# Diagonal products of a state-space scan at full width: scaled x padded with zeros, two heads adding to one place

## What is computed

```python
xdt = xf * dtc[..., None]
decay = segsum_decay(a_cum)
cb = jnp.einsum('bclgn,bcsgn->bcgls', cc, bc)
y_diag = jnp.einsum('bcgls,bcgrls,bcsgrp->bclgrp', cb, decay, xdt)
...
y_off = jnp.einsum('bclgn,bcgrpn,bcgrl->bclgrp', cc, prev, jnp.exp(a_cum))
return (y_diag + y_off).reshape(b, l, h, p)
```

## Time and profile before

| | us |
|---|---|
| median of three runs | 1126.25 (1126.03 to 1126.39) |
| the profiled execution | 1126.33 |
| its span, first to last instruction | 1124.6 |
| TensorE busy | 1114.9 (99%) |
| VectorE busy | 859.2 (76%) |
| ScalarE busy | 565.1 (50%) |
| GpSimd busy | 38.4 (3%) |

### The profile page before, as it was taken

One profiled execution on the slowest core, in us unless ns is written; L12 is line 12 of the kernel. 1 busy time (PEld: TensorE's weight loads), 2 busy tenths in 40 slices (PEclk: granted clock), 3 DMA queues, 4 the chain that ended last, 5 costly groups with the idle time before them and its releaser, 6 DMA issues.

```text
span 1124.6 us, 15412 instructions
## 1 busy us (share of the span) xinstructions
PE 1114.9 (99%) x6378; PEld 968.7 (86%) x6378; DVE 859.2 (76%) x1011; ACT 565.1 (50%) x650; POOL 38.4 (3%) x93
## 2 busy tenths in 40 slices
PE   8999999999999999999999999999999999999997
PEld 7888888888888998899899888899899899888886
DVE  6778889999854798999998524598999999983325
ACT  5666676767533654454444322474545444442323
POOL 7000000000100000000000000000000000000000
PEclk9999999999999999999999999999999999999999
DMA  8244343443232332323323344212223323333221
GB/s 277 76 133 133 129 132 131 131 132 131 76 112 77 111 112 77 112 75 119 107 75 122 109 158 147 82 38 76 94 75 113 112 76 113 112 103 120 78 75 75
DMA packets 85414, 122.07 MB, mean 109 GB/s; under 512 B 4216, under 2 KB 71392, under 8 KB 85345
## 3 DMA queue, kind: packets, MB, share of 16 engines
q1 hardware_dynamic: 85162, 121.02, 32.8%
q10 hardware_dynamic: 182, 0.07, 0.0%
HBM read 118.92 MB, written 2.16 MB: 108 GB/s over the span
## 4 chain that ended last, share of the span: by engine, by line
PE 99%; DVE 0%; issue 0%; POOL 0%; ACT 0%; DVEq 0%; POOLq 0%
PE bank L1077 29%; PE bank L344 18%; PE bank L346 18%; PE bank L345 18%; PE bank L552 6%; PE bank L838 1%; PE bank L829 1%; PE bank L790 1%; PE bank L468 1%; PE bank L780 1%; PE bank L1460 1%; PE bank L1475 0%; PE bank L492 0%; PE bank L1477 0%; PE bank L1476 0%; PE bank L758 0%
## 5 line engine op out<-in xcount | busy, mean ns | idle before, releaser
L344 PE MATMUL bank<-h_hi,w_hi 128*128 128x512 f32 (+1 forms) x856 | 313.7, 366 | 0.0
L346 PE MATMUL bank<-h_hi,w_lo 128*128 128x512 f32 (+1 forms) x856 | 310.6, 363 | 0.0
L345 PE MATMUL bank<-h_lo,w_hi 128*128 128x512 f32 (+1 forms) x856 | 310.5, 363 | 0.0
L314 DVE TENSOR_TENSOR w_lo<-raw,w_hi 128x2048 fp32r<-128x2048 f32 x90 | 206.1, 2290 | 17.2 <-ACT w_hi L309 16.0
L309 ACT ACTIVATE w_hi<-raw 128x2048 fp32r<-128x2048 f32 x90 | 172.0, 1911 | 66.8 <-PE bank L346 65.9
L346 PEld LDWEIGHTS bank<-h_hi,w_lo 128*128 128x128 f32 x856 | 161.5, 189 | 25.9
L344 PEld LDWEIGHTS bank<-h_hi,w_hi 128*128 128x128 f32 x856 | 161.7, 189 | 25.0 <-issue 0.8
L345 PEld LDWEIGHTS bank<-h_lo,w_hi 128*128 128x128 f32 x856 | 161.8, 189 | 24.4
L571 DVE SCALAR_TENSOR_TENSOR tmp<-bank,par,tmp 128x511 f32<-128x511 f32 (+1 forms) x176 | 129.4, 747 | 17.3 <-ACT tmp L562 13.6
L1077 PE MATMUL bank<-w_hi,dn_hi 128*128 128x512 f32 x348 | 107.6, 390 | 0.0
L1440 DVE TENSOR_TENSOR dn_lo<-gated,dn_hi 128x1024 fp32r<-128x1024 f32 x22 | 26.9, 1224 | 105.4 <-ACT dn_hi L1436 105.4
(11 more groups left out here) (230 smaller groups left out, 1610.5 us busy)
## 6 DMA issues: line engine op xcount, KB each, us to landing
raw<-in_ffn_w_up SPq DMA_DIRECT2D x44, 1024.0 KB, 5.1
raw<-in_ffn_w_down SPq DMA_DIRECT2D x22, 1024.0 KB, 5.1
raw<-in_ssd_w_in SPq DMA_DIRECT2D x19, 1024.0 KB, 5.4
decay<-ac_dram SPq DMA_DIRECT2D x16, 512.0 KB, 5.2
raw<-in_ssd_w_out SPq DMA_DIRECT2D x8, 1024.0 KB, 5.0
from_start<-ac_dram SPq DMA_DIRECT2D x32, 128.0 KB, 4.5
xres<-in_x SPq DMA_DIRECT2D x4, 512.0 KB, 5.8
result<-xres SPq DMA_DIRECT2D x3, 512.0 KB, 2.6
```

The lines of the kernel that those rows point to most:

```text
L314: dve.tensor_tensor(lo[:], raw[n % 2][:], hi[:].bitcast(F32), ALU.subtract).then_inc(lo_ready, 1)
L344: pe.matmul(dst, wh, xh, start=first, stop=False, **kw)
L345: pe.matmul(dst, wh, xl, start=False, stop=False, **kw)
L346: return pe.matmul(dst, wl, xh, start=False, stop=last, **kw)
```

## The change

The tile `xdt` gets twice the columns: per chunk 256 in place of 128. Of these, columns 0 to 63 are head 0's scaled x, 64 to 191 stay zero, 192 to 255 are head 1's. A stationary operand is now 128 columns wide: head 0's x beside 64 zeros, or 64 zeros beside head 1's x. Each product writes all 128 partitions, and the second head's is added to the first's. GpSimd clears the middle columns once, behind its constants; VectorE waits for that before it writes pair 0. `heads_in` moves to another place in the memory, under `group_scale`.

```diff
-            xdt = sb("xdt", [P, T], scope=scope)
+            xdt = sb("xdt", [P, NCH, 2 * P], scope=scope)
...
+            with ExitStack() as opening:
+                heads_in = sb("heads_in", [P, 3, HEADS], scope=opening)
...
-            heads_in = sb("heads_in", [P, 3, HEADS], scope=scope)
...
             for c in range(NCH):
                 for h in range(2):
-                    mm = pe.matmul(bank[h * HD:(h + 1) * HD, YD_BANK, cs(c)],
-                                   xdt[:, c * P + h * HD:c * P + (h + 1) * HD], decay[:, p % 2, h, cs(c)],
-                                   start=True, stop=True)
+                    mm = pe.matmul(bank[:, YD_BANK, cs(c)], xdt[:, c, h * P:(h + 1) * P], decay[:, p % 2, h, cs(c)],
+                                   start=h == 0, stop=h == 1)
             mm.then_inc(yd_mm, 1)
...
+            if p == 0:
+                dve.wait_ge(xdt_clear, 1)
-            dve.tensor_tensor(xdt[:, :].rearrange("p (c h d) -> p c h d", h=2, d=HD), tok,
+            dve.tensor_tensor(xdt[:, :, :].rearrange("p c (q d) -> p c q d", d=HD)[:, :, 0:4:3, :], tok,
                               dt[:, :, heads].unsqueeze(3).to_broadcast([P, NCH, 2, HD]),
                               ALU.mult).then_inc(xdt_ready, 1)
...
             pool.sem_inc(win_ready, 1)
+            pool.wait_ge(tr_done, 8)
+            pool.memset(xdt[:, :, HD:3 * HD], 0.0).then_inc(xdt_clear, 1)
```

More of the change, by code:

```diff
@@ L231, in hybrid_trunk @@
         st_mm, st_step, states_ready = sem("st_mm"), sem("st_step"), sem("states_ready")
-        x_tok_mm, xdt_ready, xde_ready = sem("x_tok_mm"), sem("xdt_ready"), sem("xde_ready")
+        x_tok_mm, xdt_clear, xdt_ready, xde_ready = sem("x_tok_mm"), sem("xdt_clear"), sem("xdt_ready"), sem("xde_ready")
         diff_ready, relu_ready, exp_ready, m_ready = sem("diff_ready"), sem("relu_ready"), sem("exp_ready"), sem("m_ready")
```

## The result

| kernel | median (lowest to highest), us | against the kernel before, 95% interval |
|---|---|---|
| before | 1126.18 | |
| changed | 1134.37 (1134.16 to 1134.66) | 1.0073 (1.0062 to 1.0083) |

The change makes the kernel slower by 8.2 us or 0.73%. Both medians are of six executions. The direction was forecast, and so was the mechanism in the scan.

A forecast was written before the change was run, and what follows sets the result against it. TensorE's start-to-start steps were taken to bound the kernel. Fifteen pairs of heads at +0.61 us (9.15) plus 0.56 for the last pair made 9.7 us, so 1136.0 us, with a range of 1134.5 to 1138.5 at 90%.

The forecast's parts named there:

- The bound: Whole kernel: TensorE, busy 99% of the 1124.6 us span, sets the time by its start-to-start steps.
- Part 1, the products: Scan, each pair of heads: sixteen full instructions replace eight couples, +0.91 us, borders -0.30, net +0.61; fifteen pairs 9.15 us.
- Part 2, the last pair: Last pair of heads, followed by output products instead of transposes: 2.91 us instead of 2.35, so +0.56.
- Part 3, adding: Second head's products written onto the first head's place: nothing added.
- Part 4, the padded write: VectorE's scaled x, same 512 elements in two blocks: 0.69 us as before, at most 1.38, unseen by TensorE.
- Parts 5 and 6: GpSimd's clearing memset, at most 0.84 us, and VectorE's wait, 49 us of cover: no cost; moved tiles change only addresses: nothing.
- the sum: Whole kernel: 9.15 + 0.56 = 9.7 us, all on TensorE and in series, giving a time of 1136.0 us.
- full products in one part each: Scan products: fewer instructions, 0.29 us less a pair of heads, 4.6 us faster, 1121.7 us; chance 2%.
- closer together: Scan products: 22 full ones in a row pack to near 0.074 us, no change, 1124 to 1128.5 us; chance 3%.
- a stall where heads add: Scan products: second head waits for the first's to land, 10.2 us more, 1146.2 us; chance 4%.
- VectorE as the bound: Scan: VectorE falls behind if the scaled x is over 1.6 us dearer, perhaps 1140 us; chance 1%.

## Right and wrong, step by step

*The bound* (TensorE, start to start): right. TensorE waits nowhere in the scan, in any of the kernels.

*Part 1, the products*: right up to the next block product. 0.61 us from the first state product to there was forecast and measured, the gain of the borders included. The same sum without them would have been 0.91 x 16 = 14.6 us. That the count of instructions stays at 256 was right too.

*Part 2, the last pair*: +0.57 for +0.56.

*Part 3, adding*: free, now shown by the kernel that leaves it out.

*Part 4, the padded write*: 0.69 us a write as before, and no shift within the scan in the kernel that has all but the width. *Parts 5 and 6*, as far as TensorE is concerned: right.

*What failed* is the step in part 5 that costed VectorE's new wait at nothing, and with it the sum's "all in series with the rest, since nothing behind the scan waits for anything but TensorE". The earlier trace rows lists TensorE's own waits and can't show what the end waits for: that is SyncE, 2.8 us for the store. I asked who waits for that instruction and found 49 us of cover. I didn't ask what one instruction more does to the instruction stream itself. With it the last load of instructions comes ahead of the last store of the result instead of among its packets, and 1.1 us is gone, some 1050 us after the wait. That is 1.1 of the 1.5 us between the 9.7 forecast and the 8.2 measured. The kernel with TensorE waiting in VectorE's place has the same scan and takes 1135.43 us, 9.3 more than its kernel before.

*A smaller miss* is the 0.45 us that the block products behind the transposes give back, a term of part 1 that stood at nothing. It could be read in the timeline of the kernel before, just behind the earlier trace rows: 184.77 to 187.39 is 2.62 us for eleven steps, and the eleven from 187.62 to 190.11 take 2.49, which leaves 2.62 - 2.49 - 0.09 (the longer first step) = 0.04. I had put the end of the border at the first block product, and it reaches some ten products further. It goes with the border and not with the length of the pair. Twelve steps from the first product of that block take 2.84 to 2.86 us in the nine traces with narrow products, even where the pair of heads is longer by 0.49 or 0.87, and 2.81 or 2.82 in the three with full ones.

*The range* was too narrow on the low side. It took its width from the price of one product, which was known best, and left 1 us below for everything else. Without the tail the measured 8.2 would have been 9.3, so 1135.5, inside it.

*The rivals*: full products in one part each (2%), closer together (3%), a stall where heads add (4%) and VectorE as the bound (1%) are all refuted by the steps of 0.111 and the absence of waits. The Trainium skill's 81 ns for a load and a product of 128 columns ("TensorE: Matmul & The Clock Gate", Back-to-back issue gap) is not what fp32 shows in any kernel here: 111 ns, also for twenty-two in a row. Its rule that a change of the tiling mode drains ("TensorEngine Tiling (Array Packing)", Key Properties) agrees with all orders that were tried, as each of them pays at its borders; that it is a drain the traces don't show.

## A kernel that beats both

The kernel before with one more wait on VectorE, for something long done, takes 1125.17 us. That is 1.3 less than the kernel before beside it (0.9989, 0.998 to 0.9999), and 1.0 less than the median of 1126.18 beside the result. It is no improvement in the work. It shows that 1 us of the kernel before hangs on where a load of instructions happens to fall. Other edits of VectorE's stream could move it again; only this one was tried.

## What to carry to other kernels

Read what a pair of narrow products costs from starts, not durations: two that use different halves of TensorE's columns and stand next to each other cost one, and padding them with zeros to full width pays the border back but not the second product. Where a kernel's end waits for a store, look for the loads of instructions among its packets, and keep a microsecond of the range for an edit that changes only the number of instructions. When comparing two variants, take the last product's start and the tail apart before giving the difference to the edit.

## What the runs showed of the hardware

- An fp32 product of 128 by 128 is issued in two parts, each 0.111 us from start to start; at 64 columns each part costs 0.109. Two parts in different halves of the columns cost 0.109 together when the halves alternate.
- Going from full to narrow products and back costs 0.30 us, and 0.03 more over the next ten products. Two other orders cost 0.03 and 0.06 more; none of the neighbours tried makes it free.
- With the halves in two groups of eight parts, seven steps around the change of half are 0.055 us long and the others 0.11, so parts of the two halves come together over a few instructions, not only as next neighbours.
- Where a load of 8 KB of instructions, 0.31 us of one DMA engine, fell among the last packets of the result's last store, the store landed 3.0 to 3.1 us after its issue; where the load came first, after 2.0. The Trainium skill, "Runtime: NRT & Kernel Launch", Instruction fetch mechanics, says that a sequencer fetches its next block through a DMA queue of its own, at a cost that is mostly hidden. A queue of instructions is in the traces (q14), though they don't say whose. Here the cost was most likely not hidden, as the load met the one transfer on which the end hangs. Of the 1.1 us, 0.54 is the later last packet; the other 0.56, behind that packet, is open.
